# A two-block transformer kernel on one core: the factor of a norm put on after the product, dummy products between units, and the order of one pair of units

## The reference, cut to what matters

```
x = x + rwkv7_time_mix(rms_norm(x, a_norm))            # first block, layer 0
x = x + short_conv_mix(rms_norm(x, b_norm))            # first block, layer 1
x = rms_norm(x, final_norm)                            # end of the first block
# second block
h    = rmsnorm(x, norm_mix_pre)
proj = h @ w_in                                        # 1024 -> 4608 columns
conv_in, q, k, v, g_conv, g_att = split(proj)
u    = a * sigmoid(b)   with a, b the halves of conv_in  (glu, 512 columns)
u    = silu(layernorm(depthwise_conv(u, 31 taps)))
att  = stick_breaking_attention(q, k, v)
mix  = (sigmoid(g_conv)*(u@w_conv+b) + sigmoid(g_att)*(att@w_att)) @ w_out
x    = x + rmsnorm(mix, norm_mix_post)
ff   = (silu(h@w_gate) * (h@w_up)) @ w_ffn_down,  h = rmsnorm(x, norm_ffn_pre)
x    = x + rmsnorm(ff, norm_ffn_post)
```

## Time and profile before

| what | value |
|---|---|
| median of 3 runs | 2197.27 us (2197.24 to 2198.46) |
| the profiled execution's own time | 2199.01 us |
| its span in the profile | 2197.3 us |
| PE busy | 2049.6 us, 93% of the span |
| DVE, ACT busy | 1416.5 us (64%), 995.4 us (45%) |
| the chain that ended last | PE 82%, DVE 9%, ACT 5%, issue 3% |
| lines 1680 to 1682 in that chain | 23%, 22%, 22% |

### The profile page before, as it was taken

How to read it: one execution, slowest core, us unless ns; L and a number is a source line. 1 busy time by engine, 2 the same in 40 slices (tenths; PEclk the granted TensorE clock), 3 DMA queues, 4 the chain that set the end, 5 groups by cost and what they waited for, 6 DMA issues and landing times.

```text
span 2197.3 us, 43117 instructions
## 1 busy us (share of the span) xinstructions
PE 2049.6 (93%) x16706; PEld 1632.8 (74%) x16706; DVE 1416.5 (64%) x2261; ACT 995.4 (45%) x1751; POOL 169.5 (8%) x183
## 2 busy tenths in 40 slices
PE   5999999978888887999999999999899989999997
PEld 4877777767777775888888888778566867887875
DVE  7778888866666664355654555688885655445355
ACT  6656666636665655232222223332666234333243
POOL 5120000012322223000000000000000000000000
PEclk9999999989999998999999999999999989999998
DMA  4445555633333311333233333233112312333332
GB/s 119 120 137 172 175 175 172 177 93 81 86 85 92 71 33 68 96 87 104 86 101 91 96 95 94 78 93 99 37 40 76 97 57 86 99 92 91 95 87 81
DMA packets 395950, 215.16 MB, mean 98 GB/s; under 512 B 85137, under 2 KB 374313, under 8 KB 395817
## 3 DMA queue, kind: packets, MB, share of 16 engines
q1 hardware_dynamic: 395608, 213.18, 33.6%
q10 hardware_dynamic: 208, 0.06, 0.0%
HBM read 181.68 MB, written 31.52 MB: 97 GB/s over the span
## 4 chain that ended last, share of the span: by engine, by line
PE 82%; DVE 9%; ACT 5%; issue 3%; SPq 1%; DMA 1%; ACTq 0%; DVEq 0%
PE bank L1680 23%; PE bank L1681 22%; PE bank L1682 22%; PE bank L565 3%; PE bank L542 1%; PE bank L573 1%; PE bank L474 1%; PE bank L488 1%; PE bank L516 1%; DVE w_lo L1927 1%; PE bank L495 1%; ACT inv L717 1%; PE bank L554 1%; PE bank L1800 1%; PE bank L508 1%
## 5 line engine op out<-in xcount | busy, mean ns | idle before, releaser
L1680 PE MATMUL bank<-xl,w_hi 128*128 128x512 f32 x1680 | 673.1, 401 | 22.2 <-DVE w_lo L1927 8.3
L1681 PE MATMUL bank<-xl,w_lo 128*128 128x512 f32 x1680 | 660.8, 393 | 0.0
L1682 PE MATMUL bank<-xl,w_hi 128*128 128x512 f32 x1680 | 659.1, 392 | 0.0
L1357 ACT ACTIVATE w_hi<-w_raw 128x1024 fp32r<-128x1024 f32 x280 | 294.2, 1051 | 358.5 <-PE bank L1682 357.8
L1927 DVE TENSOR_TENSOR w_lo<-w_raw,w_hi 128x1024 fp32r<-128x1024 f32 x280 | 343.3, 1226 | 118.7 <-ACT w_hi L1357 112.5
L1680 PEld LDWEIGHTS bank<-xl,w_hi 128*128 128x128 f32 x1680 | 317.4, 189 | 122.2 <-issue 42.0
L1682 PEld LDWEIGHTS bank<-xl,w_hi 128*128 128x128 f32 x1680 | 317.1, 189 | 71.4
L1681 PEld LDWEIGHTS bank<-xl,w_lo 128*128 128x128 f32 x1680 | 317.7, 189 | 66.8 <-issue 2.2
L1680 PE MATMUL bank<-xh,w_hi 128*128 128x512 f32 x480 | 198.1, 413 | 15.7 <-DVE xh L1932 13.9
L1681 PE MATMUL bank<-xh,w_lo 128*128 128x512 f32 x480 | 189.8, 395 | 0.0
L1682 PE MATMUL bank<-xh,w_hi 128*128 128x512 f32 x480 | 189.5, 395 | 0.0
(11 more groups left out here) (357 smaller groups left out, 2922.5 us busy)
## 6 DMA issues: line engine op xcount, KB each, us to landing
w_raw<-in_a_w_in SPq DMA_DIRECT2D x64, 512.0 KB, 4.2
w_raw<-in_b_w_in SPq DMA_DIRECT2D x64, 512.0 KB, 4.1
w_raw<-in_w_ffn_up SPq DMA_DIRECT2D x44, 512.0 KB, 4.0
w_raw<-in_w_in SPq DMA_DIRECT2D x36, 512.0 KB, 3.8
w_raw<-in_a_w_out SPq DMA_DIRECT2D x16, 512.0 KB, 4.0
w_raw<-in_b_w_out SPq DMA_DIRECT2D x16, 512.0 KB, 3.9
w_raw<-in_w_ffn_down SPq DMA_DIRECT2D x16, 512.0 KB, 3.9
d_g<-sq SPq DMA_DIRECT2D x16, 256.0 KB, 2.3
```

The source lines that it names most:

```text
L1357: A(w_hi[0:rows, slot, 0:nkb, 0:ncol], w_raw[0:rows, slot, 0:nkb, 0:ncol], ACT.Copy).then_inc(s_hi, 1)
L1680: mm(outp, wh, xlo, start=start, stop=False)
L1681: mm(outp, wl, xhi, start=False, stop=False)
L1682: return mm(outp, wh, xhi, start=False, stop=stop)
```

## The change

- The last `even` before U_GLU also makes split tiles of `xT2` times the gains (`both_gains`), without the factor per token, in `xl[2]`: ACT the high part, DVE the low part, tile by tile.
- U_GLU to U_GLU+3 run on these tiles, and the sum of squares `norm(2)` stands on PE behind the first of them. DVE puts the factor on as it reads their banks (`glu_value`, `glu_gate`), in place of ACT's copy. The tiles with the factor (`xh`), which the later units need, are made by DVE and ACT during these four units (`glu_tiles`, `glu_high`). `norm(3)` follows on PE behind U_GLU+3.
- The gates are made in `sq` instead of `rstd`, since `rstd` holds the factor. `TAPS_GLU` becomes (0,0,0), (0,0,0), (4,4,2), (4,5,2): 21 taps for 23.
- The final norm's factor has a tile of its own, `r_final`, and `final_norm(k)` runs within `even` of U_WOUT2 (`each`), once per unit.
- ACT's squares of the feed-forward part stand one tile behind the high parts; `w_high(U_FFN+2)` stands ahead of `norm(5)`, and `w_low(U_FFN+2)` ahead of the first reading of a bank.
- `spin(n)` issues n float32 products 128x128 by 128x128 on PE into a bank that nothing reads: 8 ahead of `norm(4)`, 18 behind it, 7 ahead of `norm(6)`, 12 behind it.

```diff
-TAPS_GLU = [(0, 0, 0), (2, 2, 0), (3, 4, 2), (4, 4, 2)]
+TAPS_GLU = [(0, 0, 0), (0, 0, 0), (4, 4, 2), (4, 5, 2)]
...
 # ScalarE
-                even(base + 4 * KB, DK // 2, *((xT2, 2) if half else ()))
+                if half:
+                    even(base + 4 * KB, DK // 2, xT2, 2, hi=xl[2], gain=lambda k: both_gains[:, k:k + 1])
+                else:
+                    even(base + 4 * KB, DK // 2)
...
             ahead(U_GLU, 2, 0, 0)
+            ahead(U_GLU, 2, 0, 1)
             norm(2)
-            for k in range(DK):
-                x_high(X_H3 + k, xh[:, 0, k, :], k % 2)
+            glu_high(0, 1)
+            ahead(U_GLU, 2, 1, 0)
+            glu_high(2)
+            glu_sigmoid(0)
+            glu_high(3, 4)
+            ahead(U_GLU, 2, 1, 1)
+            glu_high(5, 6)
+            ahead(U_GLU, 2, 2, 0)
+            glu_high(7)
+            glu_sigmoid(1)
             norm(3)
...
-            for k in range(DK):
-                act.wait_ge(s_mg, k + 1)
-                A(xl[0][:, 0, k, :], xT2[:, k, :], ACT.Copy, scale=col("norm_ffn_pre_2", k)).then_inc(s_xhi, 1)
-                act.wait_ge(s_sqa, squares(5) + k - 1)
-                A(sq[:, k % 2, :], xT2[:, k, :], ACT.Square).then_inc(s_sq, 1)
+            for k in range(DK + 1):
+                if k < DK:
+                    act.wait_ge(s_mg, k + 1)
+                    A(xl[0][:, 0, k, :], xT2[:, k, :], ACT.Copy, scale=col("norm_ffn_pre_2", k)).then_inc(s_xhi, 1)
+                if k:
+                    act.wait_ge(s_sqa, squares(5) + k - 2)
+                    A(sq[:, (k - 1) % 2, :], xT2[:, k - 1, :], ACT.Square).then_inc(s_sq, 1)
+            ahead(U_FFN, 2, 0, 1)
             norm(5)
...
 # TensorE
-            norm(2)
-            norm(3)
+            def spin(count):
+                for n in range(count):
+                    c = n % 4
+                    mm(bank[6][:, c * P:(c + 1) * P], ident[:], mean_d[:], start=True, stop=True)
...
-            two_units(U_GLU, xh, X_H3)
-            phase(U_GLU, 2, CT + 3 * AT // 2, xh, X_H3, started=True)
+            phase(U_GLU, 2, 2, xl[2], X_U, then=lambda: norm(2))
+            norm(3)
+            phase(U_GLU + 4, 2, CT - 2 + 3 * AT // 2, xh, X_H3)
...
+            spin(8)
             norm(4)
+            spin(18)
...
+            spin(7)
             norm(6)
+            spin(12)
...
 # VectorE
-            norm(2, lambda k: both_gains[:, k:k + 1], split(X_H3, xh, DK), xT2)
...
+            def glu_value(j):
+                dve.wait_ge(s_unit, U_GLU + 2 * j + 1)
+                V.tensor_tensor(glu[:, j, PAD2:], bank[0][:], r_glu, ALU.mult).then_inc(s_free[0], 1)
+            def glu_gate(j):
+                z = sq[:, j % 2, :]
+                dve.wait_ge(s_unit, U_GLU + 2 * j + 2)
+                if j < 2:
+                    V.tensor_tensor(z, bank[1][:], r_glu, ALU.mult).then_inc(s_free[1], 1)
+                    dve.wait_ge(s_free[1], U_GLU // 2 + j + 1)
+                    V.tensor_scalar(z, z, CLAMP, None, ALU.max).then_inc(s_gz, 1)
+                else:
+                    V.tensor_scalar(z, bank[1][:], CLAMP, None, ALU.max).then_inc(s_free[1], 1)
...
+            w_low(U_GLU + 1, 1)
+            o(V.memset(glu[:, :, 0:PAD2], 0.0))
+            w_low(U_GLU + 2, 0)
+            dve.wait_ge(s_rs, 2 + NT)
+            glu_value(0)
+            glu_tiles(0, 1, 2)
+            glu_gate(0)
+            w_low(U_GLU + 3, 1)
+            glu_tiles(3)
+            glu_product(0)
+            glu_tiles(4)
+            glu_value(1)
+            w_low(U_GLU + 4, 0)
+            glu_tiles(5, 6)
+            glu_gate(1)
+            glu_tiles(7)
+            w_low(U_GLU + 5, 1)
+            glu_product(1)
...
-            even(U_WOUT2, DK // 2, mixed, False, n=4)
+            dve.wait_ge(s_rs, 3 + NT)
+            even(U_WOUT2, DK // 2, mixed, False, n=4, each=final_norm)
...
-                    if not first:
-                        w_low(n0 + 1, 1)
+                    w_low(n0 + 2 if first else n0 + 1, 0 if first else 1)
                     dve.wait_ge(s_unit, n0 + 1)
                     dve.wait_ge(s_rs, 5 + NT)
                     V.tensor_tensor(rstd[:, 0, :], bank[0][:], r_ffn, ALU.mult).then_inc(s_free[0], 1)
                     dve.wait_ge(s_free[0], t + (base // 2 + 1))
                     V.tensor_scalar(tmp[:, 1, :], rstd[:, 0, :], CLAMP, None, ALU.max).then_inc(s_ug, 1)
-                    w_low(n0 + 2, 0)
+                    if not first:
+                        w_low(n0 + 2, 0)
```

More of the change, by code:

```diff
@@ L91 @@
 X_YC = X_H2 + DK
-X_H3 = X_YC + CI
+X_U = X_YC + CI
+X_H3 = X_U + DK
 X_AT = X_H3 + DK
@@ L105, in made @@
         return None
-    return q + 1 - CI - CI - DK
+    return q + 1 - CI - CI - 2 * DK
 def panel_dmas(n):
@@ L1538, in _ @@
             even(U_OUT1, DK // 2)
-            even(U_OUT1 + DK, DK // 2, xT2, 1, hi=xl[2], gain="b_norm")
+            even(U_OUT1 + DK, DK // 2, xT2, 1, hi=xl[2], gain=lambda k: col("b_norm", k))
             for half in range(2):
@@ L1573, in _ @@
                 ahead(U_GLU, 2, j, 1)
-                act.wait_ge(s_free[1], U_GLU // 2 + j + 1)
-                sigmoid(rstd[:, j % 2, :]).then_inc(s_glu, 1)
+                glu_sigmoid(j)
             for n in range(3 * AT):
@@ L2095, in _, with even @@
                                 ALU.subtract).then_inc(s_xlo, 1)
-            def even(base, turns, dst, add, n=None, final=False, low=None, gain=None, x0=None):
+            def even(base, turns, dst, add, n=None, final=False, low=None, gain=None, x0=None, each=None):
                 if n is not None:
@@ L2112, in turn @@
                             dve.wait_ge(s_xhi, 2 * t + (x0 + u + 1))
-                            V.scalar_tensor_tensor(out=low[:, 1, part, :], in0=where, scalar=col(gain, 2 * t + u),
+                            V.scalar_tensor_tensor(out=low[:, 1, part, :], in0=where, scalar=gain(2 * t + u),
                                                    in1=low[:, 0, part, :].bitcast(F32), op0=ALU.mult,
@@ L2124, in turn @@
                             V.tensor_tensor(acc[:], acc[:], sq[:, u, :], ALU.add).then_inc(s_sqa, 1)
+                        if each is not None:
+                            each(2 * t + u)
                 repeat(dve, turns - final, turn)
@@ L2141, in _ @@
             even(U_OUT1, DK // 2, xT2, True)
-            even(U_OUT1 + DK, DK // 2, xT2, True, n=1, low=xl[2], gain="b_norm", x0=X_H2)
+            even(U_OUT1 + DK, DK // 2, xT2, True, n=1, low=xl[2], gain=lambda k: col("b_norm", k), x0=X_H2)
             o(V.memset(cu[:, 0:2], 0.0))
@@ L2188, in _ @@
                     V.memset(acc2[:], 0.0).then_inc(s_sqb, 1)
-                even(base + 4 * KB, DK // 2, xT2, True, n=2 if half else None)
-            w_low(U_GLU + 1, 1)
-            o(V.memset(glu[:, :, 0:PAD2], 0.0))
-            norm(2, lambda k: both_gains[:, k:k + 1], split(X_H3, xh, DK), xT2)
+                    even(base + 4 * KB, DK // 2, xT2, True, n=2, low=xl[2],
+                         gain=lambda k: both_gains[:, bass.ds(k, 1)], x0=X_U)
+                else:
+                    even(base + 4 * KB, DK // 2, xT2, True)
             def final_norm(k):
-                dve.wait_ge(s_rs, 3 + NT)
-                V.scalar_tensor_tensor(out=xT2[:, k, :], in0=xT2[:, k, :], scalar=col("final_norm", k), in1=acc[:],
-                                       op0=ALU.mult, op1=ALU.mult).then_inc(s_xn, 1)
+                part = bass.ds(k, 1)
+                V.scalar_tensor_tensor(out=xT2[:, part, :], in0=xT2[:, part, :], scalar=col("final_norm", k),
+                                       in1=r_final[:].unsqueeze(1), op0=ALU.mult, op1=ALU.mult).then_inc(s_xn, 1)
             def taps():
@@ L2230, in _ @@
                 more(TAPS_GLU[j][1])
[L2231 to L2234 removed]
+                glu_gate(j)
                 more(TAPS_GLU[j][2])
[L2236 to L2238 removed]
+                glu_product(j)
             for n in range(3 * AT):
```

51 lines of the change are left out of this document (33 added, 18 removed).

## The result

The changed kernel takes 2180.57 us (median of 4 runs, 2173.21 to 2181.28) where the kernel before takes 2197.26 (4 runs): ratio 0.9911, interval 0.9895 to 0.9928. On a second chip the same pair gave 0.9896 (0.9865 to 0.9927).

What follows compares the result with a forecast made beforehand. The prediction took PE, busy 93% of the span, as the bound, with time to win only where it idles or runs at lower clock; -9.6 - 3.5 - 0.3 = -13.4 us from 2197.27 gave 2183.9 us, range 2181.5 to 2189.3.

Steps and rivals of the forecast that it cites:

- part 1: Glu units: U_GLU follows the out projection at once, U_QKV+1 starts earlier; -9.6 us, bounds -10.1 and -6.5.
- part 2: norm(4) and the U_FFN pair: dummy products hold the clock, new order shortens a stall; -3.5 us, bounds -4.8 and +1.
- part 3: The end, around norm(6): last transposes perhaps at full clock; -0.3 us, bounds -0.9 and 0.
- the margin forecast: Glu units: DVE makes w_lo(U_GLU+5) by about 1437 to 1438, wanted at 1438.8; fits by 1 to 2 us.
- rival B: DVE becomes the bound of the glu units, 3 us late at U_GLU+5: -10.3 in all, 2187.0 us; chance 0.15.
- the prediction's sum for U_QKV+1: Start of U_QKV+1: PE free at 1460.9, its low part ready at 1461.3, against 1470.98 before.
- Rival A: Dummy products don't hold the clock around norm(4) and the pair: -8.6 in all, 2188.7 us; chance 0.15.
- C: Dummy products don't overlap their weight loads and overrun the gaps: +15.8, 2213.1 us, slower than before; chance 0.03.
- D: Early tiles aren't early, PE still idles ahead of U_GLU: part 1 about half, -8.8 in all, 2188.5 us; chance 0.05.

Runs made afterwards that it cites:

- u1: Changed kernel with the 64 bytes of neg_ka placed behind w_lo instead of ahead of w_raw, same instructions: 2188.99 us, ratio 0.9932 to the kernel before.
- r3: Kernel before with only row_sum and row_rstd moved behind hT, so xx, xh, xl and hT lie 64 bytes lower: 2189.97 us, ratio 0.9951.
- r1: The kernel before, unchanged, run again: 2199.52 us, ratio 0.9996.
- s2: r3 with a pad of 32 bytes ahead of w_raw, so weights and activations move together: 2184.97 us, ratio 0.9941 to the kernel before.
- s4: Changed kernel without its four spin calls (45 dummy products): 2179.59 us, ratio 0.9918 to the kernel before.
- s1: r3 with a pad of 32 bytes ahead of xx: 2215.25 us, ratio 1.0079 to the kernel before.
- t1: r3 with a pad of 128 bytes ahead of xx: 2216.21 us, ratio 1.0076 to the kernel before.
- t4: Changed kernel with one tap less ahead of U_QKV+1's low part (TAPS_GLU's last row 4, 4, 2): 2177.89 us, ratio 0.9889 to the kernel before.

## Why the prediction was wrong

The three parts, first at one pitch (u1 against the kernel before), then at the other (changed kernel against r3), with the whole stretch between:

| step | forecast | u1 - before | changed - r3 |
|---|---|---|---|
| part 1, to U_QKV+1 | -9.6 | -9.45 | -8.0 |
| between, to the end of U_WOUT2 | 0 | +1.0 | +0.8 |
| part 2, to U_FFN+5 | -3.5 | -3.4 | -3.6 |
| part 3, the end | -0.3 | 0.0 | -0.9 |

**The step that failed is the sum.** The terms "-9.6 - 3.5 - 0.3 = -13.4 us" are three, and the change had four parts. The diff moves two tiles ahead of xx behind hT, and I gave that line no price and no bound, not even "nothing": I read it as book-keeping for `r_final`'s room. With all three bounds good the terms give -10.1 - 4.8 - 0.9 = -15.8, so 2181.5 us (the prediction wrote 2182.0 there), and the measured time lies below even that. r3 shows that the line alone gives 0.9951, about -11 us; u1 shows the other three without it at 0.9932 (0.9913 to 0.9950), which is -15.0 us, between -19.1 and -11.0, and holds the forecast of -13.4. The two ratios multiply to 0.9883, within the interval of the changed kernel's 0.9896 and below that of its 0.9911 (0.9895 to 0.9928); each factor is uncertain by about 0.002, so the ratios alone don't prove that the two add up. The profiles are clearer. Outside the recurrence, from the first `w_lo` to the last instruction, the kernel before takes 1737.6 us (r1), u1 1727.0 and the changed kernel 1716.0: 10.6 us from the edits, 11.0 from the placement, 21.6 together, 8 more than forecast. (The 10.6 is less than the parts' sum in the table, 11.9, mainly because of the 1.5 us that u1 loses in the 14 units at the pitch of 0.2333.) The first medians differ by less, 16.7 us; their runs spread over 8 us, about what the recurrence does by itself.

Part 1 was right in size and mostly in mechanism. U_GLU follows at once and the clock stays at 1.00. U_QKV+1 starts 51.9 us after U_GLU (forecast "some 52"), late by one low part: 0.76 us of idle time, forecast some 0.4. DVE kept up by the margin forecast, "1 to 2 us": the low part of U_GLU+5 ended at 1425.95, and its unit started at 1427.71. So rival B didn't come. The eight tiles under the out projection cost nothing (PE busy throughout), nor did two taps and final norms elsewhere delay U_FFN's pair. (In the prediction's sum for U_QKV+1, 1461.3 became 1461.4, a slip of 0.1.) In the changed kernel at the new distance the part is worth only 8.0 against r3, because r3's glu stretch has 6.8 us at half clock where the kernel before has 10.2 (s2, at r3's pitch, has 10.2 too and takes 61.70 us, 9.6 more than the changed kernel).

Part 2 was right: sum 1.13 us (forecast 1.02), a product 0.23 (0.25), 0.86 us idle ahead of U_FFN+2 (0.7) and U_FFN+3 late by 1.1 (1.3) for its low part. Rival A fell, the clock was held. The order is worth 0.8 us and the products 2.9.

Part 3 is 0.0 for -0.3, at the edge of its bounds; against r3 it is -0.9. The reason given was half right: the clock was up for the first tiles and down again for the last ones. The early ones don't count, since the last eight start 12.2 us behind the sum either way, by DVE's pace. What I missed is the sum ahead of them, which the kernel before ran at full clock in its profile and r3 didn't. The Trainium skill's sentence in "TensorE: Matmul & The Clock Gate", Part 4 (PE-mode transpose), that the full clock doesn't engage for transposes is not what happened after dummy products (0.66 us for four at clock 1.00, 1.11 in s4); from the third tile on, with transposes alone, the clock was down again; the time it gave for the end was nevertheless the right one.

Rivals C and D fell with the same rows. What I had not put among the rivals at all was a change of every matmul's pace.

## What to carry to other kernels

Price every line of a diff, and the ones that allocate above all: an edit that shifts tiles can change the pace of all matmuls, whatever else it is for. After any change, compare the starts of long stretches of untouched matmuls, in more than one place; if the pitch differs, the change's own gain must be measured at one and the same placement. Then fill the waits on PE that let the clock fall, but only where something behind waits for PE: the same kind of dummy products gave 2.9 us ahead of the pair and nothing ahead of the last transposes.

## What the runs showed of the hardware

The pace of 512-column matmuls at full clock depends on where tiles lie. In the stretch of 192 it follows the distance in bytes between the stationary and the moving tiles: 0.2267 us at 33,792 and at +256, 0.2289 at +64, 0.2333 at +32 and +128, with weights and activations moved together by 32 or 64 bytes changing nothing. In 14 other units of u1 it was 0.2333 at +64, so something beside this distance counts too. Why is not shown: no run separates loads of weights, reads of activations and the accesses of other engines. At half clock no such difference was seen: successive starts are 0.427 us apart in all fourteen profiles, the slow placements s1 and t1 among them.

Around a wait of about 2 us the clock sometimes drops to 0.50 for 3.4 us: in t4 1.3 us after the restart, in the changed kernel's attention by the restart itself (the four products of 1532.79 took 2.08 us, in r3 1.13). In identical code it drops in some executions and not in others. And the recurrence, whose code no edit touched, took from 438 to 455 us, and PE's waits from 420 to 860 us (in total, times, longest) differ by more than a microsecond in one row. First the changed kernel, then t4:

```profile
PE bank L570 <- issue: 17.1, 24, 2.7
```

```profile
PE bank L570 <- issue: 28.4, 27, 2.7
```

"Issue" means that the profile shows nothing that PE waited for, so the cause stays open.
